# Moving half of the adaLN features out of the input stage and beside the first projection units

## The chip, the cores and the metric

The kernel runs on one core of one Trainium2 chip. The metric is device time in microseconds, the median of several runs; a profiled execution gives the trace. TensorE multiplies (weights are loaded into it 128x128 at a time), VectorE and ScalarE work elementwise, GpSimd does so too, and SyncE (SP in the rows) issues nearly all transfers between DRAM and SBUF.

## The reference, cut to what matters

One decoder layer over 2,048 prompt tokens and 64 sample tokens (8 sequences of 8), model width 1,024. What the change touches is the first two steps:

```
shift, scale, gate = split(silu(c) @ w_ada + b_ada, 3)
h = rmsnorm(x, norm_gain) * (1 + scale) + shift      # c: one row for the prompt, 8 for the samples
u = h @ w_in                                         # 72 tiles of 128 columns
```

The columns of `u` go to dilated attention (q, k, v, z), to a gated recurrence (query, forget, input, z) and to two gates; then come the two branches, a merge and an output projection.

## The kernel before, in words

Four stages follow each other, each a block of its own in which every engine has its own queue, with a barrier between blocks: `phase_input`, `phase_weave`, `phase_mix`, `phase_tail`. The token columns are cut in a first half (0 to 1023) and a second half (1024 to 2111, the last 64 of them samples). SBUF holds the features of one half, split in two parts each (`h_high`, rounded, and `h_low`, the rest), so that a product in fp32 is made of three fast ones.

`phase_input` (line 45) makes the vectors and all features. TensorE multiplies 24 tiles of `w_ada` (512 KB each, five buffers, `load_w`) by the activated `c`: 16 tiles for shift and scale (`mod`), 8 for the gate (`gate_ps`). In between it makes the sums of squares (`sums`, L153) of a chunk of tokens. The six chunks are the second half's three first (they are written to DRAM as `h_half` and their place in SBUF is used again), then the first half's three. A chunk's way: load, `square` on ScalarE, two pair additions on VectorE (`added`, L245 and L247), the sum over partitions on TensorE, logarithm and exponential (`root`), `normed` on VectorE, `modulated` (eight steps, L259, once `mod` is there; L263 and L265 for the samples), `high` on ScalarE (L202), and the low part, half on GpSimd (L228) and half on VectorE (L271). SP loads chunk 3 only when chunk 0 has its low parts, and the last three `w_ada` tiles stand behind those loads in its queue.

`phase_weave` (line 312) does the projection. It goes through units: a unit is one weight tile (or two for rows) by up to 512 tokens, 24 matmuls (L680 to L682) in one of three banks. In the first half, units 0 to 7 and 12 to 19 are of the kinds query, forget and z, which need a curve: VectorE `clamp` (L1020), ScalarE exponential and logarithm (L843, L845), VectorE `larger` (L1025), ScalarE `sigmoid` (L850), VectorE `leave_curve` (L1034 to L1038). Units 8 to 11 are rows (48 matmuls of 256 columns, one VectorE copy). `leave_curve` of a unit stands in VectorE's queue ahead of the next unit's `clamp`. Weights come in pairs of tiles, four pieces of 256 KB a pair: SP loads a piece into one of three buffers, ScalarE casts its high part (L817), GpSimd subtracts for the low part (L921). Pieces for the next pair are split beside a pair's first three units (two, one, one). TensorE waits for the whole pair (`w_low_done`) at its first unit, and for the bank of three units earlier (`evac_done`). The recurrence joins from unit 28 on; its buffers (`q_neg`, `f_sb`, `v_sb`, `keys` and others) are idle before. At the half's end the second half's features are loaded back from `h_half`.

At the block's start SP issues seven constants, then the weight pieces; VectorE waits for all constants, then makes small tables; GpSimd first clears the semaphores of the stage before; TensorE waits for `ones_split` and the constants.

## Time and profile before

| what | us |
|---|---|
| median of 3 runs | 3144.12 (3141.14 to 3145.24) |
| the profiled execution's own time | 3146.13 |
| its span, first to last instruction | 3144.3 |
| TensorE busy in the span | 2896.0 (92%) |
| VectorE, ScalarE, GpSimd busy | 1322.7, 1077.5, 820.1 |
| mean granted TensorE clock | 0.941 |

The span is what the trace covers; the execution's own time has about 2 us more around it. Times in the rows below count from the span's start. PE is TensorE, PEld its weight loads, DVE VectorE, ACT ScalarE, POOL GpSimd; what stands in brackets at a row's end is the idle time before it and what ended it. PEclk is the granted clock as a share of 2.4 GHz.

### The profile page before, as it was taken

Reading aid. Unit: us, or ns where it says so; the run is one execution under the profiler, and the core shown is the slowest. Engines: PE = TensorE matmul, PEld = TensorE weight load, DVE = VectorE, ACT = ScalarE, POOL = GpSimd, SP = SyncE. Lnnn points to the kernel's source line nnn. Section 1 sums busy time; section 2 is a strip of 40 time slices with the busy share of each in tenths; the row PEclk is TensorE's granted clock in tenths of the full one; section 3 lists DMA queues with packets and bytes.
Section 4 is the critical chain, followed back from the end, with each engine's and each line's share of the span. In section 5 each row is a group of like instructions: output and inputs, shape, how many; then the busy total and the mean of one; then the engine's idle time right before and its main releaser. Section 6 shows DMA issues by size and latency. Waiting matters only on the chain. (4 is left out here: it accounts for less than half of the span.)

```text
span 3144.3 us, 46944 instructions
## 1 busy us (share of the span) xinstructions
PE 2896.0 (92%) x17964; PEld 2598.6 (83%) x17964; DVE 1322.7 (42%) x3014; ACT 1077.5 (34%) x2109; POOL 820.1 (26%) x690
## 2 busy tenths in 40 slices
PE   7479999999999899999999999995979898579999
PEld 6468999888888799999999999994656666379999
DVE  2623234665444323233564655432434343433433
ACT  1233212444444434212444444432535444230110
POOL 0231223555422212223554542220011112040000
PEclk7589999999999999999999999997989797799999
DMA  6522432333332342323223332226676867363432
GB/s 189 198 93 87 125 94 73 103 98 104 102 105 86 113 169 85 121 75 95 88 89 115 94 107 94 82 90 236 232 259 209 278 233 238 103 208 113 123 122 88
DMA packets 341583, 417.89 MB, mean 133 GB/s; under 512 B 62705, under 2 KB 252401, under 8 KB 334705
## 3 DMA queue, kind: packets, MB, share of 16 engines
q1 hardware_dynamic: 334448, 406.23, 40.2%
q10 hardware_dynamic: 6912, 8.65, 0.8%
q8 instruction: 144, 2.36, 0.3%
q14 instruction: 79, 0.64, 0.1%
HBM read 284.11 MB, written 130.70 MB: 132 GB/s over the span
## 5 line engine op out<-in xcount | busy, mean ns | idle before, releaser
L680 PE MATMUL weave_bank<-h_high,weave_w_high 128*128 128x352 f32 (+2 forms) x2240 | 813.8, 363 | 45.0 <-POOL weave_w_low L921 31.0
L682 PE MATMUL weave_bank<-h_high,weave_w_low 128*128 128x352 f32 (+2 forms) x2240 | 793.7, 354 | 0.0
L681 PE MATMUL weave_bank<-h_low,weave_w_high 128*128 128x352 f32 (+2 forms) x2240 | 793.5, 354 | 0.0
L921 POOL TENSOR_TENSOR weave_w_low<-weave_w_raw,weave_w_high 128x512 fp32r<-128x512 f32 x288 | 380.2, 1332 | 797.6 <-ACT weave_w_high L817 795.7
L680 PEld LDWEIGHTS weave_bank<-h_high,weave_w_high 128*128 128x128 f32 x2240 | 425.6, 190 | 83.4 <-issue 46.8
L681 PEld LDWEIGHTS weave_bank<-h_low,weave_w_high 128*128 128x128 f32 x2240 | 426.0, 190 | 35.8 <-issue 2.9
L682 PEld LDWEIGHTS weave_bank<-h_high,weave_w_low 128*128 128x128 f32 x2240 | 425.0, 190 | 36.3
L692 PE MATMUL weave_bank<-weave_w_high,h_high 128*128 128x256 f32 x1088 | 311.6, 286 | 0.0
L693 PE MATMUL weave_bank<-weave_w_low,h_high 128*128 128x256 f32 x1088 | 307.9, 283 | 0.0
L694 PE MATMUL weave_bank<-weave_w_high,h_low 128*128 128x256 f32 x1088 | 307.9, 283 | 0.0
L1613 ACT ACTIVATE mix_probs<-mix_scores,mix_o_out 128x256 f32<-128x256 f32 (+1 forms) x384 | 156.6, 454 | 318.3 <-DVE mix_o_out L1696 306.4
L843 ACT ACTIVATE weave_out<-weave_out 128x352 f32<-128x352 f32 (+1 forms) x160 | 89.1, 557 | 480.5 <-DVE weave_out L1020 480.5
L933 POOL TENSOR_TENSOR weave_sq_low<-weave_sq,weave_sq_high 128x512 fp32r<-128x512 f32 (+2 forms) x120 | 138.3, 1152 | 366.1 <-DVE weave_sq_high L990 364.9
L1020 DVE TENSOR_SCALAR weave_out<-weave_bank 128x352 f32<-128x352 f32 (+1 forms) x160 | 95.6, 597 | 325.0 <-PE weave_bank L682 324.2
L1696 DVE CUSTOM_DVE_ANT_0 mix_scores<-mix_s_head,mix_dist 128x256 f32<-128x256 f32 (+1 forms) x384 | 126.9, 364 | 226.1 <-PE mix_s_head L1482 214.3
L1503 PE MATMUL mix_o<-mix_v,mix_probsT 128*128 128x65 f32 x1200 | 168.9, 281 | 47.8 <-DVE mix_o_out L1703 47.5
L693 PEld LDWEIGHTS weave_bank<-weave_w_low,h_high 128*128 128x128 f32 x1088 | 208.9, 192 | 0.6 <-issue 0.5
L692 PEld LDWEIGHTS weave_bank<-weave_w_high,h_high 128*128 128x128 f32 x1088 | 208.7, 192 | 0.6 <-issue 0.5
L694 PEld LDWEIGHTS weave_bank<-weave_w_high,h_low 128*128 128x128 f32 x1088 | 208.8, 192 | 0.0
L1503 PEld LDWEIGHTS mix_o<-mix_v,mix_probsT 128*128 128x128 f32 x1200 | 160.5, 204 | 52.5 <-issue 49.6
L817 ACT CAST weave_w_high<-weave_w_raw 128x512 fp32r<-128x512 f32 x288 | 167.9, 609 | 90.4 <-PE weave_bank L694 56.0
L871 ACT ACTIVATE weave_d<-weave_d 128x512 f32<-128x512 f32 (+1 forms) x144 | 84.6, 588 | 254.3 <-DVE weave_d L1091 240.0
(189 smaller groups left out, 4724.3 us busy)
## 6 DMA issues: line engine op xcount, KB each, us to landing
weave_w_raw<-in_w_qkv SPq DMA_DIRECT2D x144, 256.0 KB, 3.1
mix_kv<-in_kT_c SPq DMA_DIRECT2D x24, 1024.0 KB, 7.5
mix_kv<-in_v_c SPq DMA_DIRECT2D x24, 1024.0 KB, 7.0
tail_gates<-scratch_gates SPq DMA_DIRECT2D x48, 352.0 KB, 3.2
weave_w_raw<-in_w_b SPq DMA_DIRECT2D x64, 256.0 KB, 3.0
weave_w_raw<-in_w_g SPq DMA_DIRECT2D x64, 256.0 KB, 2.9
scratch_sums<-mix_o_out SPq DMA_DIRECT2D x48, 264.0 KB, 6.1
mix_rows<-scratch_sums SPq DMA_DIRECT2D x24, 528.0 KB, 6.9
```

The source lines that it names most:

```text
L680: pe.matmul(dst, w_high[:, i, k, :], h_high[:, k, tok], start=(k == 0), stop=False)
L681: pe.matmul(dst, w_high[:, i, k, :], h_low[:, k, tok], start=False, stop=False)
L682: mm = pe.matmul(dst, w_low[:, i, k, :], h_high[:, k, tok], start=False, stop=(k == KD - 1))
L692: pe.matmul(dst, h_high[:, k, lo:lo + P], w_high[:, i:i + 2, k, :], start=(k == 0), stop=False)
L693: pe.matmul(dst, h_high[:, k, lo:lo + P], w_low[:, i:i + 2, k, :], start=False, stop=False)
L694: mm = pe.matmul(dst, h_low[:, k, lo:lo + P], w_high[:, i:i + 2, k, :], start=False, stop=(k == KD - 1))
L817: act.copy(w_part(w_high, p), w_raw[p % RAW][:, :, :]).then_inc(w_high_done, 1)
L921: pool.tensor_tensor(w_part(w_low, p), w_raw[p % RAW][:, :, :], w_part(w_high, p), ALU.subtract).then_inc(w_low_done, 1)
L933: pool.tensor_tensor(sq_low[:, 0:w], sq[:, 0:w], sq_high[:, 0:w], ALU.subtract).then_inc(sq_low_done, 1)
L1503: mm = pe.matmul(o_ps[:, h, :], probsT[n % 2][:, 2 * h + b, :], v_sb[a % 2][:, i + b - 1, h, :], start=(b == first), stop=(b == 1))
L1613: act.activation(probs[n % 2][:, h, first * P:], scores[n % 2][:, h, first * P:], ACT.Exp, scale=-1.0, bias=o_out[a % 2][:, i, h * 66 + 65 ...
L1696: dve.tensor_tensor_reduce(scores[n % 2][:, h, first * P:], s_ps[h][:, first * P:], dist[a % 2][:, h, first * P:], 1.0, 3.0e38, ALU.add, A ...
```

## The change

The input stage makes the features of the first half only (three chunks), and none is stored to DRAM from there. It also loads and splits the four pieces of the first weight pair; their loads stand in SP's queue between `w_ada` tiles 15 and 16. `w_high`, `w_low`, `mod` and `ones_d` live on into the weave. There the second half's 1,088 tokens are made in 17 groups of 64, each one step a unit from unit 0 on: load (six groups ahead of the constants, the others one a unit), square at unit f, pair sums and the sums on TensorE at f+1, root at f+2, three VectorE steps at f+3, cast and low part at f+4, two stores at f+5. The groups use the recurrence's idle buffers. TensorE no longer waits for the constants ahead of its first unit.

```diff
 phase_input, sync:
-                for n in range(9, MOD + WBUF):
+                for n in range(9, MOD):
                     load_w(n)
-                for c in range(XBUF, TCH):
-                    load_x(c)
-                    store_h(c - XBUF)
-                for n in range(MOD + WBUF, TILES):
+                for p in range(PIECES):
+                    src = dr["w_b"][0, p // 2]
+                    sp.dma_start(w_raw[p][:, :, :], src[:, 4 * (p % 2):4 * (p % 2) + 4, :]).then_inc(raw_in[p], 16)
+                for n in range(MOD, TILES):
                     load_w(n)
 phase_input, scalar, ahead of high(0), and gpsimd, ahead of the low parts:
+                for p in range(PIECES):
+                    act.wait_ge(raw_in[p], 16)
+                    act.copy(w_part(t["w_high"], p), w_raw[p][:, :, :]).then_inc(w_high_done, 1)
...
+                for p in range(PIECES):
+                    pool.wait_ge(w_high_done, p + 1)
+                    pool.tensor_tensor(w_part(t["w_low"], p), w_raw[p][:, :, :], w_part(t["w_high"], p), ALU.subtract).then_inc(w_low_done, 1)
 phase_weave, sync:
+                def load_x(f):
+                    if f >= FX:
+                        sp.wait_ge(flow_done, f - FX + 1)
+                    sp.dma_start(fx[f % FX], dr["xT"][:, :, HALF + f * NS:HALF + (f + 1) * NS]).then_inc(fx_in[f % FX], 16)
+
+                def store_x(f):
+                    sp.wait_ge(flow_done, f + 1)
+                    cols = slice(f * NS, (f + 1) * NS)
+                    sp.dma_start(dr["h_half"][0, :, :, cols], f_high[f % 3]).then_inc(f_stored[f % 3], 16)
+                    sp.dma_start(dr["h_half"][1, :, :, cols], f_low[f % 3]).then_inc(f_stored[f % 3], 16)
...
-                for p in range(7):
+                for p in range(4, 7):
                     load(p)
+                for f in range(FX):
+                    load_x(f)
+                for dst, src in CONSTANTS:
+                    sp.dma_start(dst, dr[src]).then_inc(const_in, 16)
                 for U in range(len(STEPS)):
                     if U >= 2:
                         leave(U - 2)
+                    if FX <= U + 1 < FT:
+                        load_x(U + 1)
+                    if 5 <= U < FT + 5:
+                        store_x(U - 5)
 phase_weave, tensor:
+                def feature_sums(f):
+                    pe.wait_ge(ftwo_done, f + 1)
+                    if f >= 2:
+                        pe.wait_ge(fms_done, f - 1)
+                    for k in range(2):
+                        mm = pe.matmul(l_ps[f % 2][:, 0, 0:NS], ones_d[:, :], f_pair[f % 2][:, k, :], start=(k == 0), stop=(k == 1))
+                    mm.then_inc(fss_done, 1)
...
                         features(U)
+                    if 1 <= U < FT + 1:
+                        feature_sums(U - 1)
 phase_weave, scalar:
+                def feature_square(f):
...
+                    act.activation(f_sq[f % 2], fx[f % FX], ACT.Square).then_inc(fsq_done, 1)
+                def feature_root(f):
+                    act.wait_ge(fss_done, f + 1)
...
+                    act.activation(f_rstd[f % 2], l_ps[f % 2][:, 0, 0:NS], ACT.Ln, bias=t["eps"][:, 0:1]).then_inc(fms_done, 1)
+                    act.wait_ge(fms_done, f + 1)
+                    act.activation(f_rstd[f % 2], f_rstd[f % 2], ACT.Exp, scale=-0.5).then_inc(fr_done, 1)
+                def feature_high(f):
+                    act.wait_ge(fx_steps, 3 * (f + 1))
...
+                    act.copy(f_high[f % 3].bitcast(F32R), fx[f % FX]).then_inc(fhigh_done, 1)
-                for p in range(4):
-                    split_high(p)
+                act.sem_inc(w_high_done, 4)
...
                 for U in range(len(STEPS)):
+                    if 4 <= U < FT + 4:
+                        feature_high(U - 4)
+                    if U < FT:
+                        feature_square(U)
+                    if 2 <= U < FT + 2:
+                        feature_root(U - 2)
 phase_weave, gpsimd:
+                def feature_low(f):
+                    pool.wait_ge(fhigh_done, f + 1)
...
+                    pool.tensor_tensor(f_low[f % 3].bitcast(F32R), fx[f % FX], f_high[f % 3].bitcast(F32R), ALU.subtract).then_inc(flow_done, 1)
                 nc.clear_and_free_semaphores(t["used"])
-                for p in range(4):
-                    split_low(p)
+                pool.sem_inc(w_low_done, 4)
                 for U, (j, c) in enumerate(STEPS):
+                    if 4 <= U < FT + 4:
+                        feature_low(U - 4)
 phase_weave, vector:
+                def feature_pairs(f):
+                    x = f_sq[f % 2]
+                    dve.wait_ge(fsq_done, f + 1)
...
+                    dve.tensor_tensor(x[:, 0:4, :], x[:, 0:4, :], x[:, 4:8, :], ALU.add).then_inc(ffour_done, 1)
+                    dve.wait_ge(ffour_done, f + 1)
+                    dve.tensor_tensor(f_pair[f % 2], x[:, 0:2, :], x[:, 2:4, :], ALU.add).then_inc(ftwo_done, 1)
+                def feature(f):
+                    x = fx[f % FX]
+                    dve.wait_ge(fr_done, f + 1)
+                    dve.tensor_tensor(x, x, f_rstd[f % 2].unsqueeze(1).broadcast_to([P, KD, NS]), ALU.mult).then_inc(fx_steps, 1)
...
+                    dve.tensor_tensor(x, x, vector(8), ALU.mult).then_inc(fx_steps, 1)
+                    dve.wait_ge(fx_steps, 3 * f + 2)
+                    dve.tensor_tensor(x, x, vector(0), ALU.add).then_inc(fx_steps, 1)
...
                 for U in range(len(STEPS) + 1):
+                    if 1 <= U < FT + 1:
+                        feature_pairs(U - 1)
+                    if 3 <= U < FT + 3:
+                        feature(U - 3)
                     if U and is_a("curved", U - 1):
                         leave_curve(U - 1)
                     if is_a("curved", U):
                         clamp(U)
```

`FT` is 17, `FX` is 6, `NS` is 64, `KD` is 8. `vector(8)` and `vector(0)` are scale and shift of `mod`, broadcast over the group's tokens.

## Rows read from the trace of the kernel before

**Rows 1.** Busy time of each engine in four 20 us stretches, granted clock.

```profile
core 0: us, PE busy (x) PEld busy (x) DVE busy (x) ACT busy (x) POOL busy (x), PEclk, DMA share, GB/s
60.00:80.00 20.00, 20.00 (x89) 19.00 (x88) 3.58 (x3) 1.05 (x2) 0.00 (x0) 0.50 0.46 133
100.00:120.00 20.00, 2.71 (x4) 1.17 (x4) 11.19 (x6) 6.82 (x5) 4.60 (x1) 0.50 1.07 388
140.00:160.00 20.00, 8.25 (x33) 7.26 (x32) 17.36 (x20) 6.02 (x5) 4.66 (x1) 0.50 0.00 0
200.00:220.00 20.00, 20.00 (x90) 16.57 (x89) 7.62 (x12) 8.43 (x15) 5.14 (x4) 1.00 0.32 101
```

**Rows 2.** Timeline of the input stage (start us, duration us, engine, line, operation).

```profile
79.29 17.21 PE L160 MATMUL input_gate_ps<-input_c_act,input_w_ada 128*128 128x9 f32 x80
101.03 4.60 POOL L228 TENSOR_TENSOR h_low<-input_x_sb,h_high 128x1408 fp32r<-128x1408 f32 x1 [6.23 <-ACT h_high L202]
103.47 3.65 DVE L245 TENSOR_TENSOR input_x_sq<-input_x_sq 128x1408 f32<-128x1408 f32 x1 [0.85 <-ACT input_x_sq L183]
160.41 4.38 POOL L228 TENSOR_TENSOR h_low<-input_x_sb,h_high 128x1344 fp32r<-128x1344 f32 x1 [5.29 <-ACT h_high L202]
```

**Rows 3.** Timeline of the weave's first microseconds.

```profile
165.10 0.34 SPq L519 DMA_DIRECT2D weave_ones_h<-in_ones_h  x1
171.88 0.23 DVE L1208 CAST weave_ones_r<-weave_ones_h 128x128 fp32r<-128x128 f32 x1 [9.81 <-DMA weave_o_gain<-in_o_gain]
173.26 3.70 POOL L921 TENSOR_TENSOR weave_w_low<-weave_w_raw,weave_w_high 128x512 fp32r<-128x512 f32 x3 [8.46 <-ACT weave_w_high L817]
179.30 0.77 PE L680 MATMUL weave_bank<-h_high,weave_w_high 128*128 128x512 f32 x1 [31.05 <-POOL weave_w_low L921]
```

**Rows 4.** Timeline of the weave's first units, VectorE, ScalarE and GpSimd.

```profile
187.35 0.69 DVE L1020 TENSOR_SCALAR weave_out<-weave_bank 128x512 f32<-128x512 f32 x1 [7.57 <-PE weave_bank L682]
189.28 1.12 ACT L817 CAST weave_w_high<-weave_w_raw 128x512 fp32r<-128x512 f32 x2
189.41 0.69 DVE L1025 SCALAR_TENSOR_TENSOR weave_out<-weave_bank,weave_out 128x512 f32<-128x512 f32 x1 [1.36 <-ACT weave_out L845]
190.97 0.69 DVE L1036 SCALAR_TENSOR_TENSOR weave_out<-weave_bank,weave_out 128x512 f32<-128x512 f32 x1 [0.87 <-ACT weave_out L850]
192.69 0.69 DVE L1020 TENSOR_SCALAR weave_out<-weave_bank 128x512 f32<-128x512 f32 x1 [1.03 <-PE weave_bank L682]
195.30 1.29 POOL L921 TENSOR_TENSOR weave_w_low<-weave_w_raw,weave_w_high 128x512 fp32r<-128x512 f32 x1 [2.79 <-ACT weave_w_high L817]
196.14 0.74 DVE L1038 TENSOR_SCALAR weave_out<-weave_out,weave_lb 128x512 f32<-128x512 f32 x1 [0.70 <-ACT weave_out L850]
198.13 0.69 DVE L1020 TENSOR_SCALAR weave_out<-weave_bank 128x512 f32<-128x512 f32 x1 [1.25 <-PE weave_bank L682]
```

**Rows 5.** Groups by line and shape, head (count, busy us, mean ns).

```profile
L247 DVE TENSOR_TENSOR input_pair<-input_x_sq 128x704 f32<-128x704 f32 x3 | 2.7, 891 | 0.1
L263 DVE TENSOR_TENSOR input_x_sb<-input_x_sb,input_mod 128x512 f32<-128x512 f32 x1 | 0.7, 678 | 0.0
```

**Rows 6.** Timeline of TensorE around a small fp32 product.

```profile
2074.11 0.33 PE L771 MATMUL weave_kd<-weave_hsq,weave_ones_i 128*128 128x64 f32 x2
2074.51 0.34 PE L681 MATMUL weave_bank<-h_low,weave_w_high 128*128 128x384 f32 x1
2074.69 0.34 PE L682 MATMUL weave_bank<-h_high,weave_w_low 128*128 128x384 f32 x1
```

**Rows 7.** DMA queues from 679.2 to 684 us.

```profile
DMA packets 2065, 0.54 MB, mean 113 GB/s; under 512 B 2064, under 2 KB 2064, under 8 KB 2064
q1 hardware_dynamic: 2064, 0.52, 53.0%
```

**Rows 8.** Busy time in two stretches of the mixing stage.

```profile
2320.00:2340.00 20.00, 12.52 (x62) 7.30 (x64) 5.94 (x35) 4.15 (x14) 8.51 (x5) 0.64 0.67 196
2400.00:2420.00 20.00, 19.52 (x132) 12.42 (x131) 8.34 (x39) 8.42 (x19) 0.00 (x0) 1.00 0.96 325
```

More of the change, by code:

```diff
@@ L68, in phase_input @@
         gain_sb = sb("gain_sb", [P, KD], F32)
[L69 to L70 removed]
+        mod, ones_d = t["mod"], t["ones_d"]
+        w_raw = [sb(f"w_raw{i}", [P, 4, P], F32) for i in range(PIECES)]
         w_ada = [sb(f"w_ada{i}", [P, KD, P], F32) for i in range(WBUF)]
[L72 to L75 removed]
+        x_sb = [sb(f"x_sb{i}", [P, KD, CHUNK[i][1]], F32) for i in range(TCH)]
+        x_sq = sb("x_sq", [P, KD, TW], F32)
+        pair = [sb(f"pair{i}", [P, 2, TW], F32) for i in range(2)]
+        rstd = [sb(f"rstd{i}", [P, TW], F32) for i in range(2)]
         ada_ps, gate_ps = ps("ada_ps", [P, 16, 9], F32), ps("gate_ps", [P, 8, 9], F32)
@@ L80, in phase_input @@
         w_in = [sem(f"w_ada_loaded{i}") for i in range(WBUF)]
-        x_in = [sem(f"x_loaded{i}") for i in range(XBUF)]
+        x_in = [sem(f"x_loaded{i}") for i in range(TCH)]
+        raw_in = [sem(f"w_raw{i}_loaded") for i in range(PIECES)]
+        w_high_done, w_low_done = sem("w_high_done"), sem("w_low_done")
         c_done, silu_steps, silu_done = sem("c_exp_done"), sem("silu_steps"), sem("silu_done")
@@ L85, in phase_input @@
             ("sq_done", "four_done", "two_done", "ss_done", "ms_done", "r_done", "xn_done"))
-        h_done, s_done, high_done, low_a_done, low_b_done = (sem(n) for n in
-            ("h_done", "s_done", "high_done", "low_a_done", "low_b_done"))
-        h_stored = [sem(f"h_chunk{i}_stored") for i in range(3)]
+        h_done, high_done, low_a_done, low_b_done = (sem(n) for n in
+            ("h_done", "high_done", "low_a_done", "low_b_done"))
         gate, h_high, h_low = t["gate"], t["h_high"], t["h_low"]
         width = lambda c: CHUNK[c][1]
-        x_of = lambda c: x_sb[c % XBUF][:, :, 0:width(c)]
-        first = lambda c: CHUNK[c][0] % HALF
-        cols = lambda c: slice(first(c), first(c) + width(c))
-        ahead = lambda c: [s for s in range(3) if c >= 3 and first(s) < first(c) + width(c) and first(c) < first(s) + width(s)]
+        cols = lambda c: slice(CHUNK[c][0], CHUNK[c][0] + width(c))
+        w_part = lambda x, p: x[:, p // 2, 4 * (p % 2):4 * (p % 2) + 4, :]
         with nc.Block() as block:
@@ L142, in _ @@
                 sp.wait_ge(ident_in, 16)
-                for c in range(3):
-                    sp.wait_ge(h_stored[c], 32)
             @block.tensor
@@ L164, in _ @@
                 pe.wait_ge(ones_in, 32)
-                for n in range(MOD + WBUF):
+                for n in range(TILES):
                     vector(n)
@@ L168, in _ @@
                         sums(n // 4)
-                for c in range(XBUF, TCH):
-                    sums(c)
-                    vector(MOD + WBUF + c - XBUF)
             @block.scalar
@@ L197, in high @@
                     act.wait_ge(h_done, KD * (c + 1))
[L198 to L202 removed]
+                    act.copy(h_high[:, :, cols(c)], x_sb[c][:, :, :]).then_inc(high_done, 1)
                 square(0)
@@ L375, in phase_weave @@
         kd_ps, o_ps = ps("kd", [P, 4, P], F32), ps("o", [P, CH], F32)
+        flat = lambda x: x[:, :, :].rearrange("p c q -> p (c q)")
+        f_view = lambda x: x.rearrange("p (k t) -> p k t", k=KD)
+        fx = [f_view(x) for x in (q_neg[0][:, :], q_neg[1][:, :], f_sb[0][:, :], f_sb[1][:, :], flat(v_sb[0]), flat(v_sb[1]))]
+        f_high = [f_view(x) for x in (keys[:, :], k_out[:, :], flat(att))]
+        f_low = [f_view(x) for x in (x_sb[0][:, :], x_sb[1][:, :], flat(k_turned))]
+        f_sq = [f_view(x) for x in (o_sb[:, :], z_sb[:, :])]
+        f_pair = [d_sb[i][:, 0:2 * NS].rearrange("p (k t) -> p k t", k=2) for i in range(2)]
+        f_rstd = [hsq[:, 0:NS], hrstd[:, 0:NS]]
+        FT, FX = (HALF + NS) // NS, len(fx)
+        fx_in, f_stored = [sem(f"x{i}_loaded") for i in range(FX)], [sem(f"features{i}_stored") for i in range(3)]
+        fsq_done, ffour_done, ftwo_done, fss_done, fms_done, fr_done, fx_steps, fhigh_done, flow_done = (sem("features_" + n) for n in
+            ("sq_done", "four_done", "two_done", "ss_done", "ms_done", "r_done", "x_steps", "high_done", "low_done"))
         const_in, h_in = sem("const_loaded"), [sem(f"h_chunk{i}_loaded") for i in range(3)]
@@ L622, in recurrence @@
                     h, j = HSTEPS[s]
+                    if k == -5 and s == 0:
+                        for i in range(3):
+                            sp.wait_ge(f_stored[i], 32 * len(range(i, FT, 3)))
                     if k == -5 and s in (0, 2 * BH):
```

109 lines of the change are left out of this document (39 added, 70 removed).

## The prediction, made before the changed kernel ran

> **What bounds the kernel now.** I read the span by stretches first. TensorE is wall to wall from 200 us on, and for most of the first 180 us too little of it does useful work: at 100-120 and 140-160 us it is busy 2.7 and 8.3 of 20 us, at a granted clock of 0.50, the level of 1.2 GHz [rows 1]. Whatever shortens the head before the first projection unit therefore comes off the span nearly one for one, and whatever TensorE is kept from between 180 and 300 us is added one for one.
>
> Then the timeline of the head. The 16 vector tiles that the first half's features need are done at 79.3 us; GpSimd has written the first half of its low parts for chunks 0 to 2 by 105.63 (101.03 + 4.60); and chunks 3 to 5 hold the stage until 164.79 (160.41 + 4.38) [rows 2]. After it the weave block loads constants and a weight pair, splits the pair, and starts its first matmul only at 179.30 [rows 3]. So 14.5 us more go by without TensorE.
>
> Last, one unit of the weave. Its 24 matmuls take 5.44 us (a clamp at 192.69, the next at 198.13). VectorE and ScalarE answer each other: clamp, two activations, "larger" (2.75 us from 187.35 to 190.10), a sigmoid, and a last VectorE step of 0.69 [rows 4]. VectorE then waits for the unit's end; that idle second is what the change spends.
>
> **The head, taken away.** Three chunks instead of six: what is left to end the stage is the vector chain. Five gate tiles took 17.21 us from 79.29, 3.44 each; all eight then run on without the gap in which they waited behind the features' loads, to 79.3 + 8 x 3.44 = 106.8, and the gate's addition ends the stage near 107.3. The feature side is done earlier, by 105.6, with the samples' part still in it. Gain 164.8 - 107.3 = 57.5 us, 56 to 59.
>
> The first pair's loads, four casts and four subtractions move into this stage. They stand on SP's queue between vector tiles 15 and 16, so the loads of tiles 16 on pass behind 1 MB, with five tile buffers ahead. Their cover is 60-80 us, where ScalarE is busy 1.05 us and GpSimd not at all [rows 1]; uncovered, four casts and four subtractions would cost 4 x (0.6 + 1.29) = 7.6 us [rows 4]. I cost them at nothing.
>
> Calling the weave's start S (about 107.6), the first matmul waits only for GpSimd's clearing of semaphores and a count. The trace shows no time for the clearing; it is bounded by 0 and by 8.2 us (165.1 to GpSimd's first work at 173.26 [rows 3]). GpSimd was waiting for ScalarE there, not seen working, so I take 2. Gain 14.5 - 2.3 = 12.2, 6 to 14. Together 69.7.
>
> **What TensorE does more.** Seventeen feature groups of 64 columns, each with two fp32 matmuls over a 128x128 table. The same form stands in the weave: from L771 to the second projection matmul behind it 0.40 us pass, of which one ordinary spacing is 0.18, so 0.22 for one [rows 6]. 17 x 2 x 0.22 = 7.5 us, 5 to 11.
>
> **The start of the weave.** VectorE begins with a wait for all seven constants. They now stand on SP's queue behind three weight pieces and six feature loads of 1,024 packets of 256 bytes. A store of 2,064 packets under 512 bytes kept the queue busy 53.0% of 4.8 us, 2.5 us [rows 7]; a load of half as many is about 1.25. Before, VectorE's wait ended 6.8 us after the block's start (171.88 [rows 3]); now 6.8 + 6 x 1.25 = 14.3, and with the 1.5 us of small steps behind it VectorE is ready at S + 15.8. Unit 0 ends near S + 10 (it takes 8.05, 179.30 to 187.35, partly at the low clock), unit 1 at S + 15.5. TensorE's sums for group 0 follow unit 1 and need VectorE's pair sums, which stand behind clamp and larger of unit 0: S + 15.8 + 2.75 + 0.75 = 19.3. Cost 3.8 us; 0 if the loads land sooner, 8 if each 256-byte load takes twice that. Queued behind the wait are the evacuations of units 0 and 1, but three banks cover those.
>
> **VectorE's round beside units 1 to 19.** This is the step on which the sum hangs. Two rows give two-input operations by size (0.891 us for 704, 0.678 for 512 [rows 5]), so 0.41 for 256 and 0.28 for 128: pair sums 0.75 us with their gaps, the three feature steps 3 x 0.68 + 0.08 = 2.12. They stand in VectorE's order between larger of one unit and the last step of the same unit, where it would otherwise wait; but the next clamp stands behind them. The round is 2.75 + 0.75 + 2.12 + 0.72 = 6.34 against TensorE's 5.44 + 0.44 = 5.88, say 5.9. That alone is 0.46 us a unit, nearly lost in TensorE's lead: pair sums are ready 2.75 + 0.75 = 3.5 into a unit of 5.9, so 2.4 of lead.
>
> GpSimd is the other term. VectorE's operation of 1,408 elements at 103.47 took 3.65 us where its size gives 1.64 [rows 2, 5]: it stood until GpSimd's subtraction ended at 105.63. In the weave the same: a VectorE step at 196.14 stood until GpSimd's 195.30 + 1.29 = 196.59 [rows 4]. "Larger" at 189.41, with one input from PSUM, kept its 0.69. All five new VectorE operations read two SBUF operands. GpSimd issues 1.29 us for each weight piece, released when a cast ends, just ahead of the pair sums; and now one more for each group's low part, released by a cast that follows the sigmoid, in the middle of the feature steps. So nearly each GpSimd operation meets them. One meeting costs between 0 and 1.29; I take 1.0, nearer to the upper end, since the order puts GpSimd first. (The Trainium skill, SBUF — State Buffer, Who interferes with whom, says that a VectorE instruction with two SBUF inputs and a GpSimd instruction that reads SBUF exclude each other for the whole instruction; by its letter each meeting costs nearly 1.29 and the time would be 3115.)
>
> Units 1 to 3: rounds 4.22 + 2, 4.22 + 1, 6.34 + 1 = 18.8 against 17.7, late 1.1. Units 4 to 7: four rounds and eight GpSimd operations, 25.4 + 8 = 33.4 against 23.6, late 9.8; the row units 8 to 11 (no ScalarE answer in the round) take up 2.4 of it. Units 12 to 18: six rounds and 13 operations, 38.0 + 13 = 51.0 against 35.4, late 15.6 less the lead of 2.4. With the start: 3.8 + 1.1 + 9.8 - 2.4 + 13.2 = 25.5 us. At 1.29 a meeting, 25 meetings add 7.3: 33. At nothing a meeting only the start is left: 4. ScalarE's additions (square, two short steps, cast) fit in its round and are hidden by VectorE's; SP's three more transfers a unit are 3.75 us of queue in a round of 6 to 9, beside a share that the weight loads leave free.
>
> **Sum.** -69.7 + 7.5 + 25.5 = -36.7. The profiled execution took 3146.13 for a span of 3144.3; the median of the runs is 3144.12. Against the median, the same difference gives 3107.4; 3107.
>
> **Rivals.** (a) The feature work is hidden after all: GpSimd's operations fall outside VectorE's. For it speaks that VectorE is busy only 7.62 of 20 us there [rows 1]; against it the order above. -69.7 + 7.5 + 4 = -58.2: 3086. (b) Slower: TensorE, now waiting 2 to 4 us in each unit, runs at the low clock beside units 1 to 19. At 2320-2340 us it is busy 12.52 of 20 us and granted 0.64; at 2400-2420, 19.52 and 1.00 [rows 8]. At half clock a unit is 5.2 us longer with its sums, a row unit 6.2: 15 x 5.2 + 4 x 6.2 = 103, VectorE's rounds then fit inside, and -69.7 + 7.5 + 103 + 4 = +45: 3189. It decides from 12 units at the low clock on. (The Trainium skill, TensorE: Matmul & The Clock Gate, HAM oscillation, describes matmul bursts that each start cold after waiting for another engine; by that rule this rival is the case to fear. The rows show a fall in the mixing stage only, none beside the weave.) (c) More than the locks: a weight piece cast after a late clamp makes a pair late as well, or a feature load is late for its square; up to 12 us more, 3120.
>
> **Chances.** Forecast 0.70, (a) 0.17, (b) 0.05, (c) 0.08. The range 3087 to 3129 reaches half into (a) and over (c). Measurement tells 0.2%, about 6 us, from no change. All but (b) are faster: faster 0.94, same 0.01, slower 0.05.
>
> **What would show it.** The input stage ends at 107 with the gate tiles; the first weave matmul comes 2 us later; the clamps of units 4 to 7 and 12 to 18 stand 7.5 to 9 us apart instead of 5.44, and TensorE's idle time there is put down to VectorE's pair sums; VectorE's feature operations have means near 1 us instead of 0.69. If clamps stay 6 us apart, (a) is right; if matmul spacing beside the units is 0.43 instead of 0.23, (b). I am wrong if the stage ends later than 107, or if the units beyond 21 change their pace.

## The result, and the profile after

The changed kernel took 3122.79 us (median of 6 runs, 3119.76 to 3132.25), the kernel before 3144.89 beside it (6 runs, 3141.14 to 3149.8): a ratio of 0.9932, 95% interval 0.9918 to 0.9945. It is faster by 22 us (0.7%) where 37 were forecast, and inside the range. The profiled execution took 3124.32 for a span of 3122.5.

First the stretches of the changed kernel (busy time, granted clock), to be held against [rows 1].

```profile
core 0: us, PE busy (x) PEld busy (x) DVE busy (x) ACT busy (x) POOL busy (x), PEclk, DMA share, GB/s
60.00:80.00 20.00, 20.00 (x89) 19.11 (x89) 2.96 (x1) 3.19 (x6) 7.27 (x4) 1.00 0.61 185
120.00:140.00 20.00, 11.99 (x46) 9.51 (x45) 9.39 (x19) 7.45 (x15) 3.97 (x3) 0.74 0.33 83
140.00:160.00 20.00, 18.59 (x87) 14.99 (x85) 15.07 (x20) 11.10 (x23) 5.37 (x5) 1.00 0.12 45
160.00:180.00 20.00, 16.97 (x80) 13.77 (x81) 17.00 (x22) 7.80 (x16) 6.43 (x5) 0.91 0.72 185
200.00:220.00 20.00, 20.00 (x110) 17.19 (x110) 14.87 (x19) 6.49 (x16) 6.07 (x5) 1.00 0.67 169
220.00:240.00 20.00, 17.05 (x73) 13.32 (x72) 15.82 (x21) 10.93 (x23) 6.04 (x5) 0.91 0.76 187
```

TensorE is wall to wall in the head now, which ends near 110, and the idle time stands behind it: 8.0 of 20 us at 120-140 and about 3 at 160-180 and 220-240. VectorE is busy 15 to 17 us of 20 from 140 on; before it was 7.62 beside such units.

The timeline of the changed kernel from the gate tiles to the first units: the answers to [rows 2, 3], then one round of VectorE and GpSimd (units 5 and 6), the answer to [rows 4], and TensorE in that round. "..." marks rows left out.

```profile
81.85 27.46 PE L144 MATMUL input_gate_ps<-input_c_act,input_w_ada 128*128 128x9 f32 x128
82.04 0.31 DVE L245 TENSOR_TENSOR mod<-input_ada_ps,input_b_sb 128x144 f32<-128x144 f32 x1 [9.41 <-PE input_ada_ps L144]
109.35 0.23 DVE L260 TENSOR_TENSOR gate<-input_gate_ps,input_b_sb 128x72 f32<-128x72 f32 x1 [6.37 <-PE input_gate_ps L144]
110.24 0.79 PE L667 MATMUL weave_bank<-h_high,w_high 128*128 128x512 f32 x1 [0.93 <-POOLq L993]
125.10 0.23 DVE L1262 CAST weave_ones_r<-weave_ones_h 128x128 fp32r<-128x128 f32 x1 [15.52 <-DMA weave_o_gain<-in_o_gain]
126.84 0.69 DVE L1050 TENSOR_SCALAR weave_out<-weave_bank 128x512 f32<-128x512 f32 x1
129.49 1.50 DVE L1242 TENSOR_TENSOR weave_o_sb<-weave_o_sb 128x256 f32<-128x256 f32 x1
131.03 1.24 DVE L1244 TENSOR_TENSOR weave_d<-weave_o_sb 128x128 f32<-128x128 f32 x1
132.32 1.11 PE L780 MATMUL weave_l<-weave_d,ones_d 128*128 128x64 f32 x4 [8.01 <-DVE weave_d L1244]
...
163.73 0.68 DVE L1050 TENSOR_SCALAR weave_out<-weave_bank 128x512 f32<-128x512 f32 x1
165.78 0.69 DVE L1055 SCALAR_TENSOR_TENSOR weave_out<-weave_bank,weave_out 128x512 f32<-128x512 f32 x1 [1.36 <-ACT weave_out L843]
166.33 1.27 POOL L944 TENSOR_TENSOR w_low<-weave_w_raw,w_high 128x512 fp32r<-128x512 f32 x1 [5.12 <-ACT w_high L815]
166.38 1.50 DVE L1242 TENSOR_TENSOR weave_z<-weave_z 128x256 f32<-128x256 f32 x1
167.72 1.30 POOL L991 TENSOR_TENSOR weave_k_turned<-weave_f,weave_att 128x512 fp32r<-128x512 f32 x1
167.92 1.24 DVE L1244 TENSOR_TENSOR weave_d<-weave_z 128x128 f32<-128x128 f32 x1
169.22 0.66 PE L780 MATMUL weave_l<-weave_d,ones_d 128*128 128x64 f32 x4 [2.80 <-DVE weave_d L1244]
171.07 0.63 PE L669 MATMUL weave_bank<-h_high,w_low 128*128 128x512 f32 x1
171.50 0.63 PE L667 MATMUL weave_bank<-h_high,w_high 128*128 128x512 f32 x1
171.59 0.68 DVE L1050 TENSOR_SCALAR weave_out<-weave_bank 128x512 f32<-128x512 f32 x1
174.33 0.40 PE L668 MATMUL weave_bank<-h_low,w_high 128*128 128x512 f32 x1
...
175.80 1.27 DVE L1244 TENSOR_TENSOR weave_d<-weave_o_sb 128x128 f32<-128x128 f32 x1
177.12 0.66 PE L780 MATMUL weave_l<-weave_d,ones_d 128*128 128x64 f32 x4
```

The head: the gate's addition at 109.35 and the first projection matmul at 110.24, 69.06 us before that of [rows 3]. The start: VectorE waits 15.52 us for the last constant, and TensorE, done with unit 1 at 124.31, stands 8.01 us for the first pair sums. The round: clamp to clamp is 7.86 us. The two pair sums take 1.50 and 1.24 us where their sizes give 0.41 and 0.29; the first ends at 167.88, behind GpSimd's subtraction for a weight piece (to 167.60), the second at 169.16, behind the low part (to 169.02). TensorE stands 2.80 us for them. Its matmuls behind the wait come 0.43 us apart for a while (171.07 to 171.50) and take 0.63 instead of 0.40. At the end of that unit the next pair sums are ready at 177.07, and TensorE takes them up at 177.12.

What TensorE waited for from 95 to 300 us in the changed kernel (us in total, times, longest):

```profile
PE weave_l L780 <- DVE weave_d L1244: 19.9, 7, 8.0
PE weave_bank L667 <- POOL w_low L944: 1.4, 1, 1.4
PE weave_bank L667 <- POOLq L993: 0.9, 1, 0.9
```

VectorE's new operations by form, 126 to 268 us (count, busy us, mean ns), the answer to [rows 5]:

```profile
L1242 DVE TENSOR_TENSOR weave_o_sb<-weave_o_sb 128x256 f32<-128x256 f32 x9 | 12.0, 1331 | 0.0
L1244 DVE TENSOR_TENSOR weave_d<-weave_o_sb 128x128 f32<-128x128 f32 x9 | 10.3, 1149 | 0.3
L1257 DVE TENSOR_TENSOR weave_q_neg<-weave_q_neg,mod 128x512 f32<-128x512 f32 x6 | 7.3, 1223 | 0.2
L1259 DVE TENSOR_TENSOR weave_q_neg<-weave_q_neg,mod 128x512 f32<-128x512 f32 x6 | 4.2, 692 | 0.2
```

The last row is an undisturbed operation of 512 elements; the others are 1.8 to 4 times what their size gives. These groups are some of the longest (rows go by tile): over all 17 feature groups the five operations, in their order, took 1.11, 0.91, 1.00, 1.06 and 0.75 us in the mean, where their sizes give 0.41, 0.29 and three times 0.69.

### The profile page after: what moved, and what is told of

Same layout as the page of the kernel before. It is cut to its first block and busy times, and to the rows that moved or that the text cites. A ratio compares the mean times of both kernels' runs of the same rounds, so it can differ in the third digit from the quotient of the medians.

```text
span 3122.5 us, 47274 instructions
## 1 busy us (share of the span) xinstructions
PE 2919.9 (94%) x18020; PEld 2609.9 (84%) x18020; DVE 1361.6 (44%) x3061; ACT 1085.1 (35%) x2165; POOL 836.7 (27%) x704
## 5 line engine op out<-in xcount | busy, mean ns | idle before, releaser
L667 PE MATMUL weave_bank<-h_high,w_high 128*128 128x352 f32 (+2 forms) x2240 | 819.8, 366 | 15.2 <-issue 11.4
L669 PE MATMUL weave_bank<-h_high,w_low 128*128 128x352 f32 (+2 forms) x2240 | 801.4, 358 | 0.0
L668 PE MATMUL weave_bank<-h_low,w_high 128*128 128x352 f32 (+2 forms) x2240 | 799.1, 357 | 0.0
L944 POOL TENSOR_TENSOR w_low<-weave_w_raw,w_high 128x512 fp32r<-128x512 f32 x284 | 379.9, 1349 | 771.1 <-ACT w_high L815 769.2
L667 PEld LDWEIGHTS weave_bank<-h_high,w_high 128*128 128x128 f32 x2240 | 427.0, 191 | 57.5 <-issue 14.7
L669 PEld LDWEIGHTS weave_bank<-h_high,w_low 128*128 128x128 f32 x2240 | 426.0, 190 | 40.4
L668 PEld LDWEIGHTS weave_bank<-h_low,w_high 128*128 128x128 f32 x2240 | 426.0, 190 | 39.7 <-issue 2.9
L679 PE MATMUL weave_bank<-w_high,h_high 128*128 128x256 f32 x1088 | 310.0, 285 | 0.0
L681 PE MATMUL weave_bank<-w_high,h_low 128*128 128x256 f32 x1088 | 306.7, 282 | 0.0
L680 PE MATMUL weave_bank<-w_low,h_high 128*128 128x256 f32 x1088 | 305.6, 281 | 0.0
```

The costliest lines, as they stand in the source:

```text
L667: pe.matmul(dst, w_high[:, i, k, :], h_high[:, k, tok], start=(k == 0), stop=False)
L668: pe.matmul(dst, w_high[:, i, k, :], h_low[:, k, tok], start=False, stop=False)
L669: mm = pe.matmul(dst, w_low[:, i, k, :], h_high[:, k, tok], start=False, stop=(k == KD - 1))
L679: pe.matmul(dst, h_high[:, k, lo:lo + P], w_high[:, i:i + 2, k, :], start=(k == 0), stop=False)
L680: pe.matmul(dst, h_high[:, k, lo:lo + P], w_low[:, i:i + 2, k, :], start=False, stop=False)
L681: mm = pe.matmul(dst, h_low[:, k, lo:lo + P], w_high[:, i:i + 2, k, :], start=False, stop=(k == KD - 1))
```

## The stretches in which the kernels are compared

Each profile was cut at five points: TensorE's first projection matmul, three starts of VectorE's clamps (of 160 in all: that of unit 22, which is the 19th, since units 20 to 23 have clamps as well; the 41st; the last), and the span's end. "Weave start" is first matmul to clamp of unit 22; in "half 0" (19th to 41st clamp) and after it no kernel's work is changed.

| kernel | first matmul | weave start | half 0 | 41st to last clamp | last clamp to end |
|---|---|---|---|---|---|
| before | 179.30 | 128.93 | 639.27 | 1193.91 | 1002.9 |
| before, again (e7) | 182.93 | 128.26 | 639.28 | 1193.54 | 1005.3 |
| changed | 110.24 | 169.32 | 643.67 | 1191.83 | 1007.4 |
| e1, no low parts | 110.34 | 157.15 | 643.64 | 1191.00 | 1014.4 |
| e2, constants first | 109.80 | 161.68 | 643.65 | 1190.99 | 1007.2 |
| e3, steps after clamp | 110.77 | 148.06 | 643.65 | 1191.31 | 1007.2 |
| e4, low parts on VectorE | 110.36 | 161.67 | 643.68 | 1194.74 | 1009.0 |
| e5, e2 and e3 together | 110.10 | 138.62 | 643.66 | 1189.39 | 1007.9 |
| e10, the same again | 109.47 | 138.09 | 643.68 | 1189.08 | 997.0 |
| e6, old place of `h_low` | 110.20 | 171.04 | 639.96 | 1191.01 | 1002.0 |
| e9, e5 and e6 together | 110.26 | 137.12 | 639.98 | 1190.51 | 1002.3 |
| e8, e5 with the split in the weave | 128.47 | 139.16 | 643.68 | 1187.05 | 1000.2 |

Two profiles of one kernel agree within 0.7 us in the weave start, 0.02 in half 0 and 0.4 from there to the last clamp. Behind it, in code that is the same in all of them, the twelve profiles lie between 997.0 and 1014.4, and the head of the kernel before alone differed by 3.6 us. So the medians, which contain all this (the kernel before took 3151.64, 3152.83 and 3148.49 on the chips of the three sets of runs), say less of a single cause than this table; the stretches of unchanged code are no evidence for or against a cause.

From before to changed the span went 69.06 - 40.39 - 4.40 + 2.08 - 4.5 = 21.8 us, the columns in order.

## The experiments

Except e7, all edits are on the changed kernel. The first four ran on one chip, e5 to e8 on another, e9 and e10 on a third. In the expectations of e9 and e10 "unit 48" is a wrong name for the 41st clamp.

**e1, what GpSimd's low parts cost VectorE.**

```diff
-                    pool.tensor_tensor(f_low[f % 3].bitcast(F32R), fx[f % FX], f_high[f % 3].bitcast(F32R), ALU.subtract).then_inc(flow_done, 1)
+                    pool.sem_inc(flow_done, 1)
...
-                    sp.dma_start(dr["h_half"][1, :, :, cols], f_low[f % 3]).then_inc(f_stored[f % 3], 16)
+                    sp.dma_start(dr["h_half"][1, :, :, cols], f_high[f % 3]).then_inc(f_stored[f % 3], 16)
```

> The changed kernel without GpSimd's 17 subtractions for the second half's low parts: GpSimd only passes the signal on, and the high part is stored in both places, so this part of the computation is left out. If GpSimd's subtractions stop VectorE's two-operand steps (the lock theory), each round from unit 4 to 19 loses one meeting of 1.0 to 1.3 us, some 13 rounds: 12 to 17 us less than the changed kernel's 3122.8, 3106 to 3111, and the means of the three feature steps fall to 0.69. If VectorE's round is long by its own work alone, or the weights are what is late, nothing moves: 3121 to 3125.

Measured: 3111.21 us, ratio 0.9879 (0.9857 to 0.9901); weave start 12.2 us shorter. VectorE's 85 new operations took 35.1 us more than their sizes give in the changed kernel, with 35 of them over 0.25 us too long; without the low parts 20.7, with 20. TensorE's waits behind the start fell from 13.3 to 6.0 us. So GpSimd's low parts do hold VectorE up. The gain is at the lower end of what was expected, and the means of the three feature steps fell to 0.88, 0.75 and 0.69 and not all to 0.69. What is left on GpSimd in this stretch are the weight pieces' subtractions.

**e2, the constants ahead of the feature loads.**

```diff
+                for dst, src in CONSTANTS:
+                    sp.dma_start(dst, dr[src]).then_inc(const_in, 16)
+                load_x(0)
                 for p in range(4, 7):
                     load(p)
-                for f in range(FX):
+                for f in range(1, FX):
                     load_x(f)
-                for dst, src in CONSTANTS:
-                    sp.dma_start(dst, dr[src]).then_inc(const_in, 16)
```

> The changed kernel with the seven constants ahead of the feature loads on SP's queue, as in the kernel before. VectorE's first wait ends some 7 us after the weave's start instead of 15.2, so the first clamp follows unit 0 at once. If the start delay is carried through by VectorE's rounds to unit 8, TensorE's wait of 8.0 us before unit 2 goes, and with it the 1.6 us at the low clock behind it: 9 to 10 us less, 3113. If TensorE's lead takes the delay up before unit 8 anyway, 2 us less at most, 3121.

Measured: 3110.95 us, ratio 0.9867 (0.9846 to 0.9889). VectorE's wait for the last constant fell from 15.52 to 6.47 us, the first clamp came at 117.55 instead of 126.84, and the weave start is 7.6 us shorter. The stall at the start was the constants' place in SP's queue (the first feature load moved ahead of the weight pieces as well, but the wait is for the constants). It is some 2 us less than the 9 to 10 expected: unit 20 ran at the low clock in e2 (7.0 us from its first to its last matmul instead of 5.4), where VectorE's clamps had begun to wait for TensorE again. TensorE's waits in e2 and what its matmuls did behind two of them are taken up further below:

```profile
180.25 0.66 PE L781 MATMUL weave_l<-weave_d,ones_d 128*128 128x64 f32 x4 [1.81 <-DVE weave_d L1245]
183.46 0.41 PE L682 MATMUL weave_bank<-w_high,h_low 128*128 128x256 f32 x1
183.67 0.41 PE L680 MATMUL weave_bank<-w_high,h_high 128*128 128x256 f32 x1
...
238.15 0.66 PE L781 MATMUL weave_l<-weave_d,ones_d 128*128 128x64 f32 x4 [2.80 <-DVE weave_d L1245]
239.16 0.39 PE L670 MATMUL weave_bank<-h_high,w_low 128*128 128x512 f32 x1
239.38 0.39 PE L668 MATMUL weave_bank<-h_high,w_high 128*128 128x512 f32 x1
...
252.92 0.50 PE L668 MATMUL weave_bank<-h_high,w_high 128*128 128x512 f32 x1 [2.93 <-POOL w_low L945]
```

**e3, the feature steps behind the clamp.** VectorE's three steps move from the place where the next clamp stands behind them to the place where it waits for ScalarE's answer to the clamp (1.36 us idle ahead of "larger", above).

```diff
-                    if 3 <= U < FT + 3:
-                        feature(U - 3)
                     if U and is_a("curved", U - 1):
                         leave_curve(U - 1)
                     if is_a("curved", U):
                         clamp(U)
+                    if 3 <= U < FT + 3:
+                        feature(U - 3)
```

> The changed kernel with the three feature steps moved in VectorE's order from ahead of the last step of the unit before to behind the clamp, where VectorE waits 1.36 us for ScalarE. If VectorE's round sets the pace, each of 12 rounds shortens by up to that wait: 13 to 16 us less, 3107 to 3110. If it is only the locks that set the pace, the steps meet GpSimd's operations in the new place as well and little is gained: 0 to 4 us less, 3119 to 3123.

Measured: 3102.82 us, ratio 0.9852 (0.9831 to 0.9873); weave start 21.3 us shorter, and the clamps mostly 5.9 to 6.1 us apart instead of 7 to 9, some 5 us more than the 13 to 16 expected. A round of e3 in the timeline, VectorE alone:

```profile
164.08 0.69 DVE L1050 TENSOR_SCALAR weave_out<-weave_bank 128x512 f32<-128x512 f32 x1 [1.01 <-PE weave_bank L669]
164.68 0.68 DVE L1250 TENSOR_TENSOR weave_f<-weave_f,weave_hrstd 128x512 f32<-128x512 f32 x1
165.40 0.69 DVE L1257 TENSOR_TENSOR weave_f<-weave_f,mod 128x512 f32<-128x512 f32 x1
166.12 0.69 DVE L1259 TENSOR_TENSOR weave_f<-weave_f,mod 128x512 f32<-128x512 f32 x1
166.73 0.68 DVE L1055 SCALAR_TENSOR_TENSOR weave_out<-weave_bank,weave_out 128x512 f32<-128x512 f32 x1
167.33 0.94 DVE L1242 TENSOR_TENSOR weave_o_sb<-weave_o_sb 128x256 f32<-128x256 f32 x1
170.08 0.69 DVE L1050 TENSOR_SCALAR weave_out<-weave_bank 128x512 f32<-128x512 f32 x1 [0.89 <-PE weave_bank L669]
```

The same work now ends with VectorE waiting 0.9 to 1.0 us for TensorE. Its operations are still held up, by 18.3 us in 23 of them, but that lies in the slack of the round: behind the start, TensorE waits for no pair sums any more. The move also halved the delay (35.1 to 18.3), so the 21.3 us are not the sequence alone. But e1, with about as much delay left (20.7) and the steps in their old place, is 9.1 us slower than e3. So the sequence in VectorE's queue, as well as GpSimd, made the rounds long.

**e4, the low parts on VectorE**, one unit later, behind the pair sums.

```diff
-                    if 4 <= U < FT + 4:
-                        feature_low(U - 4)                        # gpsimd
...
                     if 1 <= U < FT + 1:
                         feature_pairs(U - 1)
+                    if 5 <= U < FT + 5:
+                        feature_low(U - 5)                        # vector
```

> The changed kernel with the second half's low parts subtracted on VectorE (0.69 us each, behind the pair sums) instead of on GpSimd. Lock theory: a meeting of 1.0 to 1.3 us goes and 0.72 of work comes in each of some 13 rounds: 4 to 7 us less, 3116 to 3119. If GpSimd's operations cost VectorE nothing, it is 0.72 us a round more: 9 us more, 3132.

Measured: 3109.47 us, ratio 0.9873 (0.985 to 0.9897); weave start 7.7 us shorter, where 4 to 7 were expected. VectorE does 17 operations more, 14.9 us of work (0.68 us each undisturbed, about 1.05 where a weight piece's held them up), and the rounds are shorter all the same. Held against e1, which leaves the subtractions out, they make the weave start 4.5 us longer on VectorE and 12.2 us longer on GpSimd. The delay of VectorE's other operations fell from 35.1 to 17.2 us (e1: 20.7).

**e5, e2 and e3 together.**

> Both moves together: the seven constants first on SP's queue, and VectorE's feature steps behind the clamp instead of ahead of it. Theory (the weave's start and VectorE's rounds are two separate costs, and TensorE's own pace is the floor): the clamps of units 2 to 20 stand about 6.0 us apart from the start, the first clamp falls within 8 us of the first weave matmul, first matmul to the clamp of unit 22 takes 138 to 141 us (148.1 with the second move alone, 169.3 with none), and the ratio to the kernel before is 0.982 to 0.984, some 8 us under the second move alone. Rival (the start's stall is swallowed, since TensorE is the bound of the later rounds and would catch up in any case): 146 to 148 us, within 2 us of the second move alone.

Measured: 3090.74 us (3089.71 to 3094.49), ratio 0.9816 (0.9793 to 0.9839); weave start 138.62, 9.4 us under e3 alone. The two costs are separate. What TensorE waited for in e5, 95 to 300 us:

```profile
PE weave_bank L668 <- POOLq L994: 0.9, 1, 0.9
PE weave_l L781 <- DVE weave_d L1245: 0.3, 1, 0.3
```

Of the 21.3 us of waiting behind the first matmul 0.3 is left. The 9.7 us above the kernel before's 128.93 are the 17 sums, 6.2, and some 3.5 from units of 512 columns that take 5.65 us where a sum stands behind them, and 5.57 elsewhere, instead of 5.44.

**e6, where `h_low` lies.** The change had moved it in SBUF behind `w_high`, `w_low`, `mod` and `ones_d`.

```diff
+            keep(ctx, "h_low", [P, KD, SEQ // 2 + NS], F32R)
             keep(ctx, "w_high", [P, 4, KD, P], F32R)
...
-            keep(ctx, "h_low", [P, KD, SEQ // 2 + NS], F32R)
             phase_input
```

> The changed kernel with one thing put back: h_low is kept in SBUF ahead of the weights' high and low parts, as in the kernel before. No work is changed. Placement theory (the projection units of 512 columns take 5.57 instead of 5.44 us because of where their operands lie): units 25 to 45 back at 5.44 us, and some 6 us gained by unit 88. Rival (the pace of matmuls differs from chip to chip or from run to run, or hangs on something else): units unchanged beside the control run of the same chip, ratio 0.991 to 0.995, that of the changed kernel.

Measured: 3115.16 us (3113.81 to 3116.0), ratio 0.9891 (0.9868 to 0.9913). Half 0 falls from 643.67 to 639.96 (before: 639.27), with units of 512 columns at 5.44 us again. The order in which the kept buffers were laid out cost 3.7 us of those 4.4 in a stretch where no instruction had changed. The 6 us expected by unit 88 did not come: from unit 22 to unit 88 it is 0.9, and the weave start, which VectorE's rounds set in both, was 1.7 us longer. Groups by form, the changed kernel and then e6 (busy us, mean ns), show the two sides of it: 512 columns faster, 256 columns a little slower (a row unit of 48 matmuls takes 5.65 us in the changed kernel and 5.76 in e6 and in the kernel before).

```profile
L667 PE MATMUL weave_bank<-h_high,w_high 128*128 128x512 f32 x896 | 365.9, 408 | 2.3 <-POOL w_low L944 1.4 <-POOLq L993 0.9
L679 PE MATMUL weave_bank<-w_high,h_high 128*128 128x256 f32 x1088 | 310.0, 285 | 0.0
```

```profile
L667 PE MATMUL weave_bank<-h_high,w_high 128*128 128x512 f32 x896 | 363.3, 405 | 4.1 <-POOL w_low L944 3.1 <-POOLq L993 0.9
L679 PE MATMUL weave_bank<-w_high,h_high 128*128 128x256 f32 x1088 | 312.5, 287 | 0.0
```

**e7, the kernel before once more.**

> The kernel before once more, unchanged, as a control with its own trace. If the pace of matmuls belongs to the program: 512-column units at 5.44 us and the stretch from the end of the weave to the last instruction as long as in the first profile, within 0.1%. If it belongs to the chip or the run: these differ by up to 1.2%, the amount by which unchanged code differed between the two first profiles. Ratio 1.000 within 0.002 either way.

Measured: 3150.37 us (3139.9 to 3162.71), ratio 0.9988 (0.9968 to 1.0008). Half 0 took 639.28, as the first time; so its pace belongs to the program. The stretch behind the last clamp was 2.4 us longer and the first matmul 3.6 later (`mod` at 83.41 instead of 79.48); the program is the same, so those belong to the run or the chip.

**e8, the first pair split in the weave again**, with both moves of e5 in.

```diff
 phase_input: the four loads, casts and subtractions of the first pair left out
 phase_weave, sync:
-                for p in range(4, 7):
+                for p in range(3):
                     load(p)
                 constants, then load_x(0) to load_x(5)
+                for p in range(3, 7):
+                    load(p)
 phase_weave, scalar and gpsimd:
-                act.sem_inc(w_high_done, 4)
+                for p in range(4):
+                    split_high(p)
-                pool.sem_inc(w_low_done, 4)
+                for p in range(4):
+                    split_low(p)
```

> The two moves of the run before, but the first weight pair is loaded, cast and split in the weave again instead of in the input stage. Theory (the 14.5 us between the stage's end and the first matmul were this splitting, and its move is worth 12 to 14 us): the first weave matmul comes 11 to 14 us behind the weave's start instead of 0.4, and the ratio is 0.004 higher than with both moves, some 11 us. Rival (much of it is lost again, since VectorE, the constants and the feature loads need that time anyway before unit 1's sums): first matmul as late, but the clamp of unit 22 only 3 to 7 us later than with both moves.

Measured: 3106.64 us (3100.36 to 3113.87), ratio 0.9865 (0.9837 to 0.9892), 0.0049 above e5. The input stage ended no sooner without the pair (gate's addition at 109.75; e5: 109.20), so the four loads, casts and subtractions are hidden there. The first matmul waited 18.8 us for the split (e5: 0.9), and the weave start was no shorter for it (139.16 against 138.62):

```profile
PE weave_bank L660 <- POOL w_low L938: 18.8, 1, 18.8
```

In this kernel the fourth piece stands behind the constants and feature loads in SP's queue: its buffer was free at 114.8, its load left at 121.28. Without these 6.5 us the first matmul would have come 11.7 us behind the weave's start, inside the 11 to 14 expected.

**e9 and e10, both moves with the old place of `h_low`, and both moves alone again.**

> Both moves (constants first, feature steps behind the clamp) and h_low back at its old place in SBUF. Placement theory: the stretch from the clamp of unit 22 to that of unit 48 takes 640.0 us as with the order put back alone, against 643.7 with the moves alone, and the stretch from there to the last clamp stays within 1 us of that run's 1191.0: together 3 to 5 us below the two moves alone on the same chip, ratio 0.980 to 0.981. Rival (what the order gives in one stretch it takes in another): equal to the two moves within 2 us.

> The two moves alone once more, beside the run with the order put back: 0.981 to 0.983 of the kernel before. Stretches of unchanged code before the weave and behind it may differ by some us from the first run, as they did between two profiles of the kernel before; those inside the weave within 0.2 us (643.7 us from the clamp of unit 22 to that of unit 48).

Measured: e9 3082.56 us (3081.96 to 3083.7), ratio 0.979 (0.9773 to 0.9808); e10 3091.58 (3079.07 to 3097.86), ratio 0.9825 (0.9806 to 0.9844). From first matmul to last clamp e9 took 1967.6 us, e10 1970.9 and e5 1971.7: 3.2 to 4.1 us for the order, as expected. The other 5 us between the medians are not explained by it; e10's own runs spread over 19 us. e10 kept half 0 to 0.02 us of e5, but the weave start differed by 0.5 and the stretch behind half 0 by 0.3, more than the 0.2 expected. e9 is the fastest version of the study, 2.1% under the kernel before.

## Why the prediction was right, and where its terms were off

**The head, right, with two errors that cancel.** 69.06 us against 69.7. The stage ended at 109.6 where 107.3 was forecast, a gain of 55.2 us and below my 56 to 59; I had written that I would be wrong if it ended later than 107. It comes from a later `mod` (82.04 against 79.48), which lies inside what the kernel before shows in its two profiles (79.48 and 83.41). Against that the step from the stage's end to the first matmul gained 13.9 us instead of 12.2: from the weave's first issue, 109.86, to the first matmul 0.38 us pass, GpSimd's clearing of semaphores included, where I took 2. That the split of the first pair costs nothing in the input stage is shown by e8.

**The sums on TensorE, right.** 0.36 us a group, 0.47 after a wait, 0.87 for the first, 7.4 in all against 7.5.

**The start, right in kind, less than half in size.** TensorE's wait is 8.0 us against 3.8. The constants landed at the weave's start + 15.2 (forecast 14.3) and unit 1 ended at + 14.5 (forecast 15.5); and the pair sums of the first group were held up twice, 2.8 us for the 0.75 of this term (the two meetings of that round stand in the next term, where TensorE's lead hid most of them). Behind the wait unit 2 ran at the low clock, 1.6 us more. e2 shows the cause.

**VectorE's rounds, right in kind, a little too dear.** The clamps stood 7 to 9 us apart, as forecast, and from unit 4 to unit 19 VectorE did not wait for TensorE ahead of a clamp except behind the row units. A meeting was sized right: 35 operations held up for 35.1 us, 1.0 each, where I had 25 meetings of 1.0; a GpSimd pair in a row catches two VectorE operations in a row. All 35 start 0.04 to 0.84 us behind a GpSimd operation and end 0.15 us (128 elements), 0.28 (256) or 0.55 (512) behind its end, and none lost more than 1.12 us. (The Trainium skill, SBUF — State Buffer, Who interferes with whom, has a VectorE instruction with two SBUF inputs and a GpSimd instruction that reads SBUF exclude each other for the whole instruction. The trace agrees in that none of the 35 ends ahead of GpSimd's, with 1.12 us at most where the letter gives 1.29.) After the start TensorE waited 11.9 us for pair sums and 1.4 for a weight pair, 13.3 in all, against the 21.7 of my sum (25.5 - 3.8); with three slow units (next paragraph) that stood in the place of waits it is 18.3. Which of the lead and the row units took up more than I gave them, no run separates.

**The low clock, not in the sum, and cheaper than it looks.** Rival (b) put TensorE at the low clock beside units 1 to 19 and would have decided from 12 units on. In the changed kernel it came true for four: behind the waits of 8.01, 2.80, 2.72 and 2.81 us a unit took 7.2 to 7.4 us to its end instead of 5.65, with matmuls 0.43 us apart in part of it, the spacing that the first unit of the kernel before has at a granted clock of 0.50 (179.3 to 183.6), the level of 1.2 GHz. The granted clock of these stretches is 0.74 to 0.91. Behind the waits of 1.54 and 1.79 the next unit kept its pace. The length of the wait alone does not decide it: in e2 a unit lost its pace behind 1.81 us and one kept it behind 2.80 (rows above), in e6 units lost it behind 1.81 and 1.70 and one kept it behind 2.89. (The Trainium skill, TensorE: Matmul & The Clock Gate, HAM oscillation, describes bursts of matmuls that start cold after a wait, there for a DMA. These four units agree with it, by 1.6 to 1.8 us each; the others do not.)

The four cost 6.6 us of TensorE's time, but most of it only took the place of a wait. The units behind 169.22 and 224.62 ended with VectorE's pair sums just ready (177.07 and 232.62, taken up 0.05 us later); at full pace TensorE would have stood there for the difference. Unit 18 was slow in the changed kernel and TensorE then waited 1.39 us for a weight pair; in e2 unit 18 kept its pace and that wait was 2.93, 1.54 more. Of the four, only behind the wait of 8.01 did VectorE wait for TensorE (2.88 us ahead of the clamp at 140.61), so that unit's 1.6 us came on top. In e5, where the waits are gone, the granted clock is 1.00 in every stretch from 120 to 260 us.

**The sum of the weave start.** Measured 40.4: waits 21.3, slow units 6.6, sums 7.4, and 5.1 that I had not counted at all: 4.5 from units of 512 columns with 5.65 or 5.57 us instead of 5.44, and 0.6 from a first unit with more of its matmuls 0.43 us apart. Of the slower units the place of `h_low` is a part: e9, with the old place, has 5.56 where a sum stands behind a unit and 5.44 elsewhere, and its weave start is 1.5 us shorter than that of e5. Forecast 33.0. The term most off is the start, 9.6 us with its slow unit against 3.8; that the rounds came out 3.4 us cheaper than forecast and made up for part of it is luck.

**Units beyond 21.** I wrote that I would be wrong if they changed their pace. They did: 4.40 us over half 0. e6 shows 3.7 of it to be the place of `h_low` in SBUF, an edit of the diff that I had costed at nothing without naming it. After half 0 the changed kernel is 2.1 us faster in the weave. The two pairs that differ by the place alone point opposite ways there (e6 is 0.8 us faster than the changed kernel, e9 1.1 slower than e5), so this stays open.

**The whole.** The gain fell short by 14.9 us (21.8 against 36.7): 0.6 in the head, 7.4 in the weave start, 4.4 in half 0, 4.5 behind the last clamp, less the 2.1 after half 0. The mechanism was the forecast one; the number stayed inside the range because the range was wide, not because each term was right.

**What stays open.** Why placement changes the spacing of 512-column matmuls; what drops the clock behind one wait and not behind another; and the 4.5 us behind the last clamp, which lie inside the 17 us by which unchanged code differed from profile to profile.

## What to carry to other kernels

When work moves beside a stage that TensorE bounds, write down the order of the receiving engine's queue and put the new work where that engine already waits for another's answer, not ahead of the operation that frees TensorE's next step: here the same instructions cost 21 us in one place, and in the other TensorE waited for none of them behind the start. A unit at the low clock behind a wait costs only where TensorE, and not another engine, sets the next step: read what the engine behind it is doing before adding it to the bill. Ahead of new bulk loads put the small loads for which an engine's first instruction waits (7.6 us). After a gain look at the stretches that nobody touched: a buffer's new place cost 3.7 us.

## What the runs showed of the hardware that was not expected

- The place of the operands in SBUF changes the pace of matmuls: 24 of 512 columns took 5.57 us in one layout and 5.44 in another, and 48 of 256 columns the other way, 5.65 and 5.76; over half 0 the eight kernels of one layout agree within 0.04 us (643.64 to 643.68) and the two of the other within 0.02 (639.96 and 639.98).
- In the input stage the granted clock read 0.50 in the profile of before [rows 1] and 1.00 in that of the changed kernel, at the same pace of TensorE: 17.21 us for 80 matmuls [rows 2] and 27.46 for 128, 0.215 each in both. It is no difference of the kernels: the second profile of the kernel before (e7) reads 1.00 as well, again with 17.21 us for 80, and its first seven projection matmuls, 0.43 us apart, stand under 1.00 too. The clock records of that trace begin only at 186.3 us, those of the changed kernel at 116.1; ahead of them a 1.00 shows nothing. The row of e7, for [rows 1]:

```profile
60.00:80.00 20.00, 20.00 (x88) 19.00 (x89) 3.09 (x1) 1.05 (x2) 0.00 (x0) 1.00 0.49 142
```

- An elementwise subtraction was cheaper for VectorE to do itself (0.88 us in the mean; 17 of them made the weave start 4.5 us longer than without them) than to have beside it on GpSimd (12.2 us longer).
- A VectorE operation with two SBUF inputs that starts just behind a GpSimd subtraction of 1.3 us ended 0.15 to 0.55 us behind it, by its size, in all 35 cases.
